# Seven-product blocks in all three down stages, their weight sums formed by accumulating DMAs in HBM

## The reference

```python
D_FF = 2816
...
        u_gate, u_val = jnp.split(u, 2, axis=-1)
        x = x + (jax.nn.silu(u_gate) * u_val) @ w_ffn_down[layer]
    return rms_norm(x, norm_final_w)
```

## Time and profile before

| | |
|---|---|
| median of 3 runs | 1244.31 us (1244.18 to 1244.35) |
| the profiled execution's own time | 1244.18 us |
| its span in the trace | 1242.9 us |
| PE busy | 1239.0 us, 100% of the span |
| DVE / ACT / POOL busy | 957.8 / 722.1 / 422.0 us (77% / 58% / 34%) |
| chain that ended last | PE 100% |
| DMA | 233.75 MB, 188 GB/s on average |

### The profile page before, as it was taken

One profiled execution on the slowest core, in us unless ns is written; L12 is line 12 of the kernel. 1 busy time (PEld: TensorE's weight loads), 2 busy tenths in 40 slices (PEclk: granted clock), 3 DMA queues, 4 the chain that ended last, 5 costly groups with the idle time before them and its releaser, 6 DMA issues.

```text
span 1242.9 us, 17085 instructions
## 1 busy us (share of the span) xinstructions
PE 1239.0 (100%) x6634; PEld 1061.2 (85%) x6634; DVE 957.8 (77%) x1377; ACT 722.1 (58%) x1023; POOL 422.0 (34%) x338
## 2 busy tenths in 40 slices
PE   9999999999999999999999999999999999999999
PEld 8988788888888889888888888888988888888887
DVE  6875667677887478986878888986898597888895
ACT  7755545376765365577836555546457674655552
POOL 0010012039892069377420112008746750012100
PEclk9999999999999999999999999999999999999999
DMA  9753334555555448644554554465855454555442
GB/s 360 274 195 136 136 119 169 173 199 187 197 179 201 170 170 267 214 155 176 175 210 175 183 190 162 176 220 185 289 180 193 154 174 165 203 183 190 162 166 114
DMA packets 39008, 233.75 MB, mean 188 GB/s; under 512 B 4752, under 2 KB 5392, under 8 KB 13072
## 3 DMA queue, kind: packets, MB, share of 16 engines
q1 hardware_dynamic: 38928, 232.67, 53.4%
HBM read 225.31 MB, written 1.05 MB: 182 GB/s over the span
## 4 chain that ended last, share of the span: by engine, by line
PE 100%; DVE 0%; issue 0%; POOL 0%; POOLq 0%
PE ps L657 19%; PE ps L564 18%; PE ps L566 18%; PE ps L565 18%; PE ps L662 10%; PE ps L569 6%; PE ps L583 2%; PE ps L625 1%; PE ps L624 1%; PE ps L623 1%; PE ps L725 1%; PE ps L1209 1%; PE ps L700 0%; PE ps L893 0%; PE ps L810 0%; PE ps L811 0%
## 5 line engine op out<-in xcount | busy, mean ns | idle before, releaser
L1299 ACT ACTIVATE whi<-raw 128x2048 fp32r<-128x2048 f32 (+1 forms) x212 | 400.2, 1891 | 115.0 <-PE ps L566 101.5
L2052 DVE TENSOR_TENSOR wlo<-raw,whi 128x2048 fp32r<-128x2048 f32 x168 | 388.0, 2315 | 90.0 <-ACT whi L1299 89.3
L1885 POOL TENSOR_TENSOR wlo<-raw,whi 128x512 fp32r<-128x512 f32 x176 | 229.1, 1337 | 88.6 <-ACT whi L1299 85.6
L657 PE MATMUL ps<-hh,whi 128*128 128x512 f32 x1056 | 255.8, 391 | 0.0
L657 PEld LDWEIGHTS ps<-hh,whi 128*128 128x128 f32 x1056 | 193.0, 188 | 36.5
L564 PE MATMUL ps<-whi,hh 128*128 128x512 f32 (+1 forms) x504 | 201.3, 399 | 0.0
L566 PE MATMUL ps<-whi,hh 128*128 128x512 f32 (+1 forms) x504 | 195.5, 388 | 0.0
L565 PE MATMUL ps<-wlo,hh 128*128 128x512 f32 (+1 forms) x504 | 195.1, 387 | 0.0
L1857 POOL TENSOR_TENSOR st<-st,sm 128x1 f32<-128x1 f32 (+2 forms) x28 | 45.2, 1614 | 391.5 <-DVE st L2106 228.0
L662 PEld LDWEIGHTS ps<-hh,wlo 128*128 128x128 f32 x1056 | 137.8, 191 | 6.7
L662 PE MATMUL ps<-hh,wlo 128*128 128x256 f32 x1056 | 139.8, 282 | 0.0
(11 more groups left out here) (348 smaller groups left out, 2061.6 us busy)
## 6 DMA issues: line engine op xcount, KB each, us to landing
raw<-in_w SPq DMA_DIRECT2D x202, 1024.0 KB, 4.9
raw<-in_w SPq DMA_DIRECT2D x12, 256.0 KB, 6.7
gain<-in_bias SPq DMA_DIRECT2D x12, 256.0 KB, 5.0
kst<-kh SPq DMA_DIRECT2D x16, 128.0 KB, 2.8
qst<-qh SPq DMA_DIRECT2D x16, 128.0 KB, 2.3
raw<-in_w SPq DMA_DIRECT2D x2, 560.0 KB, 10.8
x<-in_x SPq DMA_DIRECT2D x4, 256.0 KB, 5.7
gain<-in_rows SPq DMA_DIRECT2D x2, 512.0 KB, 5.6
```

Of the source, the lines that this page charges most:

```text
L657: pe.op.matmul(o[:, :], wh[:, k, c], t.hh[:, k, :, :], start=k == 0, stop=False, skip_group_check=True)
L1299: act.op.activation(t.whi[i % NHI][:, c], t.raw[i % NRAW][:, c], ACT.Copy).then_inc(*at("act_hi", ("hi", i)))
L1885: pool.op.tensor_tensor(t.wlo[i % NRAW][:, half(k)], t.raw[i % NRAW][:, half(k)], t.whi[i % NHI][:, half(k)].bitcast(F32), ALU.subtract).t ...
L2052: dve.op.tensor_tensor(t.wlo[i % NRAW][:, c], t.raw[i % NRAW][:, c], t.whi[i % NHI][:, c].bitcast(F32), ALU.subtract).then_inc(*at("dve_lo ...
```

## The change

`SEVEN` becomes a tuple for each stage: chunks 2, 3, 4, 6 in dn0 (none before), 1, 2, 4, 5 in dn1 (1, 3, 5, 7 before), 1, 2, 4, 5, 6, 7 in dn2 (1, 3, 5, 7 before). That makes 14 seven-product chunks in place of 8.

The sums chunks of c = 4 in dn1 and dn2 are still added by DVE (`BY_DVE`). The other 12 (`FORMED`) are built in HBM, in a new tensor `sums`, in two batches: the seven of dn0 and dn1 while the first model runs, the five of dn2 during layer 0 of the second. For each, SP copies 1 MB of weight blocks within HBM (`blocks_copied`, two DMAs, issued ahead of the loads of chunks 16 to 22, and of the five chunks from `pa0_0` on); then POOL issues four accumulating DMAs of 128 x 512 (`first_sums`, and `later_sums` in two steps, each of which waits for the one before to land). SP later loads the finished sums chunk like a weight chunk (`load_sums`), and of the chunk itself only the last 1536 columns.

In dn0 the sums of activations are formed by DVE (`block_sums`) and split by ACT and DVE, since POOL is splitting weights in up0; in dn1 and dn2 POOL forms them as before. `sevens_added` now runs in dn0 too. The cut diff (left out: hunks that only pass `SEVEN[n]` for `SEVEN`, or move a helper):

```diff
--- before.py
+++ after.py
@@ -36,6 +36,15 @@
             plan.append((name, layer, cs, k, per))
+
+    def down(unit, name, layer):
+        n = int(unit[2])
+        units[unit] = []
+        for c in range(NFT // 2):
+            units[unit].append(len(plan))
+            plan.append((name, layer, cols((512, 512), (0, 512)) if c in SEVEN[n] else cols((0, 1024)), 2 * c, 2))
+            if c in SEVEN[n]:
+                plan.append((None, n, range(1024), 2 * c, 2))
     def in1(unit, a, n):
...
@@ -76,16 +85,12 @@
             wide(f"up{l + 1}_{f}", "w_ffn_in_2", l, cols((128 * f, 128), (FF + 128 * f, 128)), 8, 8)
-        for c in range(NFT // 2):
-            halves = cols((512, 512), (0, 512)) if c in SEVEN else cols((0, 1024))
-            units.setdefault(f"dn{l + 1}", []).append(len(plan))
-            plan.append(("w_ffn_out_2", l, halves, 2 * c, 2))
-            if c in SEVEN:
-                plan.append((None, l, range(1024), 2 * c, 2))
+        down(f"dn{l + 1}", "w_ffn_out_2", l)
     return plan, units
-SEVEN = (1, 3, 5, 7)
+SEVEN = ((2, 3, 4, 6), (1, 2, 4, 5), (1, 2, 4, 5, 6, 7))
+BY_DVE = ((), (4,), (4,))
 GATES = (4, 5, 0, 1, 2, 3)
...
@@ -279,6 +285,10 @@
 SUMS = {i for i in range(len(PLAN)) if PLAN[i][0] is None}
+FORMED = [i for i in sorted(SUMS) if PLAN[i][3] // 2 not in BY_DVE[PLAN[i][1]]]
+BATCH = [[i for i in FORMED if (PLAN[i][1] == 2) == late] for late in (False, True)]
+COPIES = {a + n: i for a, batch in zip((16, UNITS["pa0_0"][0]), BATCH) for n, i in enumerate(batch)}
+OFFS = [sum(128 * PLAN[j][4] * len(PLAN[j][2]) for j in range(i) if j not in SUMS) for i in range(len(PLAN) + 1)]
@@ -383,7 +393,7 @@
     t.gs = at("gs", p + 82, [128, 4, 128])
-    t.gsh, t.gsl = ([at(f"{w}{c}", p + o + (4, 8, 40, 30)[c], [128, 4, 128], R32) for c in range(len(SEVEN))]
+    t.gsh, t.gsl = ([at(f"{w}{c}", p + o + (4, 8, 40, 34, 30, 0, 21)[c], [128, 4, 128], R32) for c in range(7)]
                     for w, o in (("gsh", 44), ("gsl", 46)))
@@ -444,22 +454,32 @@
     at, on = ev.at, ev.on
-    offs = [0]
-    for i in range(len(PLAN)):
-        offs.append(offs[-1] + (0 if i in SUMS else 128 * width(i)))
-
     def load(sem, dst, src, *names):
             sp.wait_ge(*on("used", i - NRAW))
-        src = d["in_w"][offs[i]:offs[i + 1]].rearrange("(p n) -> p n", p=128)
+        src = d["in_w"][OFFS[i]:OFFS[i + 1]].rearrange("(p n) -> p n", p=128)
         if i < 3:
             return
-        load(f"d_raw{i % NRAW}", t.raw[i % NRAW][:, 0:width(i)], src, ("raw", i))
+        c = slice(512 if i + 1 in FORMED else 0, width(i))
+        load(f"d_raw{i % NRAW}", t.raw[i % NRAW][:, c], src[:, c], ("raw", i))
+
+    def load_sums(i):
+        sp.wait_ge(*on("used", i - NRAW))
+        sp.wait_ge(*on("sums formed", int(i in BATCH[1])))
+        load(f"d_raw{i % NRAW}", t.raw[i % NRAW][:, :], d["sums"][FORMED.index(i)], ("raw", i))
+
+    def blocks_copied(i):
+
+
+        src = d["in_w"][OFFS[i - 1]:OFFS[i]].rearrange("(p n) -> p n", p=128)
+        for h in range(2):
+            load("d_copied", d["sums"][FORMED.index(i)][:, 1024 * h:1024 * h + 1024], src[:, 512 + 512 * h:1536 + 512 * h],
+                 *([("blocks copied", int(i in BATCH[1]))] * (h and i in (BATCH[0][-1], BATCH[1][-1]))))
     def row(i):
@@ -532,7 +552,11 @@
                 stack_q(l)
-        if i not in SUMS:
+        if i in COPIES:
+            blocks_copied(COPIES[i])
+        if i in FORMED:
+            load_sums(i)
+        elif i not in SUMS:
             load_raw(i)
@@ -1085,7 +1109,7 @@
         def seven(c):
-            i, pair, edge = chunks[c], SEVEN.index(c), (SEVEN[0], SEVEN[-1])
+            i, pair, edge = chunks[c], SEVEN[n].index(c), (SEVEN[n][0], SEVEN[n][-1])
             pe.wait_ge(*on("lo", i))
...
@@ -1626,9 +1653,8 @@
                 silu(f, "scaled")
-                if f % 2 == 0 and f // 2 - 2 in SEVEN:
-                    c = f // 2 - 2
-                    upper(("g sums hi", n, c), t.gsh[SEVEN.index(c)][:, :, :], t.gs[:, :, :], ("g sums", n, c, "whole"))
+                if f % 2 == 0 and f // 2 - 2 in SEVEN[n]:
+                    sums_upper(f // 2 - 2)
                 return
@@ -1638,6 +1664,8 @@
                                   bias=fc[:, f, v, 3:4]).then_inc(*at("act_out", *([("fu biased", f)] * v)))
+            if f % 2 and (f - 3) // 2 in SEVEN[n]:
+                sums_upper((f - 3) // 2)
         def second_sums(f):
...
@@ -1886,6 +1914,31 @@
                 *at("pool_lo", *([("lo", i)] if k == 3 else [])))
+
+    def added(sem, dst, src, *names):
+        pool.op.dma_start(dst, src, accum_op=ALU.add).then_inc(*at(sem, *names, by=16))
+
+    def first_sums(late):
+
+
+        pool.wait_ge(*on("blocks copied", late))
+        for i in BATCH[late]:
+            s = d["sums"][FORMED.index(i)]
+            first = d["in_w"][OFFS[i - 1]:OFFS[i]].rearrange("(p n) -> p n", p=128)[:, 0:512]
+            for j in range(2):
+                added("d_one", s[:, half(j)], first, *([("first sums", late)] * (j and i == BATCH[late][-1])))
+
+    def later_sums(late):
+
+
+        pool.wait_ge(*on("first sums", late))
+        for i in BATCH[late]:
+            s = d["sums"][FORMED.index(i)]
+            added("d_two", s[:, half(2)], s[:, half(0)], *([("second sums", late)] * (i == BATCH[late][-1])))
+        pool.wait_ge(*on("second sums", late))
+        for i in BATCH[late]:
+            s = d["sums"][FORMED.index(i)]
+            added("d_three", s[:, half(3)], s[:, half(2)], *([("sums formed", late)] * (i == BATCH[late][-1])))
     for tt in range(2):
@@ -1899,6 +1952,7 @@
             *at("pool_small", ("kr", "rot", tt)))
+    first_sums(0)
     for k in range(4):
@@ -1906,6 +1960,7 @@
                 *at("pool_small", ("sg gained", k - 1)))
+    later_sums(0)
     for tt in range(2):
@@ -1968,8 +2023,12 @@
             norm_power(norm_before_ffn, tt)
-        for c in SEVEN:
+        if l == 0:
+            first_sums(1)
+        for c in SEVEN[l + 1]:
             g_sums(l + 1, c)
+        if l == 0:
+            later_sums(1)
     def g_sums(n, c):
...
@@ -2044,7 +2103,7 @@
             dve.wait_ge(*on("raw", i))
-            if i + 1 in SUMS:
+            if i + 1 in SUMS and i + 1 not in FORMED:
                 weight_sums(i)
@@ -2575,10 +2634,28 @@
                 dve.wait_ge(*on("g", n, f - 4))
-                if n and f % 2 == 0 and f // 2 - 2 in SEVEN:
+                if n and f % 2 == 0 and f // 2 - 2 in SEVEN[n]:
                     dve.wait_ge(*on("g sums", n, f // 2 - 2, "whole"))
                 *at("dve_out", ("fg", n, f)))
+
+        def block_sums(c):
+
+
+            k0, k1 = (t.fg[(2 * c + k) % 4] for k in range(2))
+            a11, a21, a12, a22 = k0[:, 0:128], k0[:, 128:256], k1[:, 0:128], k1[:, 128:256]
+            s3, s5, s6, s7 = (t.gs[:, j, :] for j in range(4))
+
+            def less(dst, a, b, names=()):
+                dve.op.tensor_tensor(dst, a, b, ALU.subtract).then_inc(*at("dve_small", *names))
+
+            await_own("dve_out")
+            less(s5, a21, a22)
+            less(s7, a11, a21)
+            await_own()
+            less(s6, a11, s5)
+            await_own()
+            less(s3, a12, s6, [("g sums", n, c, "whole")])
         def up_out(f):
@@ -2587,6 +2664,12 @@
                 gated(f - late)
+            if n == 0 and f % 2 and (f - 3) // 2 in SEVEN[n]:
+                block_sums((f - 3) // 2)
+            if n == 0 and f % 2 == 0 and (f - 4) // 2 in SEVEN[n]:
+                c = (f - 4) // 2
+                lower([("g sums", n, c)], t.gsl[SEVEN[n].index(c)][:, :, :], t.gs[:, :, :],
+                      t.gsh[SEVEN[n].index(c)][:, :, :], ("g sums hi", n, c), "dve_small")
             if n and 0 <= f - late - 1 < NFT:
...
@@ -2996,6 +3079,7 @@
     out = nc.dram_tensor("out_0", (S, D), _mybir.dt.float32, kind="ExternalOutput").ap()
-    program(nc, {**d, "out": out})
+    sums = nc.dram_tensor("sums", (len(FORMED), 128, CW), _mybir.dt.float32, kind="Internal").ap()
+    program(nc, {**d, "out": out, "sums": sums})
     r = _run(nc, [arrays], core_ids=[0])```

What moves, engine by engine. POOL, between the rotation of `kr` (two rows on `ra`) and the powers of the norm `n1` (the two rows on 128x1), before and of the change; `st`, `sm`, `sg`, `gnw` are small tables of statistics and gains:

```order
L1900 TENSOR_TENSOR ra_113<-ra_113,rb_115 128x512
L1857 TENSOR_TENSOR st<-st,sm 128x2 x2
L1907 TENSOR_TENSOR sg<-sg,gnw 128x1024
L1857 TENSOR_TENSOR st<-st,sm 128x2
L1907 TENSOR_TENSOR sg<-sg,gnw 128x1024
L1857 TENSOR_TENSOR st<-st,sm 128x2
L1857 TENSOR_TENSOR st<-st,sm 128x1 x2
```

More of the change, by code:

```diff
@@ L60, in chunk_plan @@
         wide(f"up0_{f}", "w_ffn_up", 0, cols((128 * f, 128), (FF + 128 * f, 128)), 8, 8)
-    wide("dn0", "w_ffn_down", 0, cols((0, 1024)), NFT, 2)
+    down("dn0", "w_ffn_down", 0)
     for l in range(2):
@@ L111 @@
     "d_third0", "d_third1", "d_third2", "d_third3",
+    "d_copied", "d_one", "d_two", "d_three",
 )
@@ L1123, in ffn @@
```

(14 more changed lines are left out.)

## The result

The changed kernel takes 1254.18 us (median of five runs, 1253.47 to 1255.06), the kernel before 1244.18 us in the same session (1243.77 to 1244.35): ratio 1.008, 95% interval 1.0068 to 1.0091. It is 10 us slower, and 13.9 us above the forecast of 1240.3.

The account below looks back on a forecast made before the run. PE, busy 100% of the span, was taken as the bound: 4.08 us saved by 18 fewer matmuls, 0.1 lost in loads, from 1244.31 to 1240.3 us. Likeliest 1240.0 to 1240.9, 8 in 10 between 1239.8 and 1243.5.

Parts of the forecast that it names:

- Matmuls: Down stages: 18 fewer matmuls on PE, four chunks' worth in dn0, none in dn1, two in dn2, saving 4.08 us.
- DVE in up0: Four groups of new DVE instructions in up0, at most 2.4 us each time, 9.5 in all, at cost 0.
- The bound of 0.42 us: In up0, each DVE instruction of 128 x 128 was taken to last below 0.42 us.
- The warning: DVE and POOL already disturb each other in up0: DVE's split takes 2.61 us there against 2.29 in dn2.
- The rule of the Trainium skill: In up0, a DVE instruction with two SBUF inputs blocks a GpSimd instruction reading SBUF until it ends; still no PE wait.
- The cover in up0: DVE idles 19 and POOL 17 of up0's 111 us; even if POOL lost 9.5 us, PE would not wait.
- Rival D: In up0, DVE and POOL delays add up in blocks 7 to 12: up to 2 us, 1241 to 1242.5; chance 0.06.
- POOL's issues (B): POOL's accumulating DMAs: cost 0 taken; rival: up1's start late if issues exceed 3.4 us each, over 1246.8 us, chance 0.10.
- Copies (C): Copies within HBM at 57 to 103 us: cost 0 taken; rival: they starve loads, 1242 to 1247 us, chance 0.07.
- the sign that the prediction named for C: ACT waiting for `raw<-in_w` between 65 and 120 us would show copies within HBM starving the loads.
- Loads in the down stages (A): Sums chunks loaded in dn0 and dn2: 0.1 us lost; rival: late loads, 1241 to 1245 us, chance 0.15.
- The limit of 7.1 us: Time left for a sums chunk's landing in the worst cases, c = 4 in dn0, c = 6 and 7 in dn2.

Follow-up runs that it names:

- e6: The changed kernel with POOL's weight splits in up0 cut from 512 to 32 columns and PE reading the upper part instead of the remainder: 1241.05 us.
- e2: The changed kernel with DVE's sums of activations in up0 moved behind the sum and scaling of the next block, same work: 1247.33 us.
- e5: The changed kernel with up0's sums formed in unused PSUM, an added ACT copy, and DVE's split of the sums moved ahead of the convolution: 1241.57 us.
- e3: The changed kernel with three of the four groups of activation sums in up0 cut to one column of 128: 1250.37 us.
- e4: The changed kernel with dn0's seven-product chunks at c = 1, 3, 5, 7 in place of 2, 3, 4, 6: 1258.24 us.

## Why the prediction was wrong, point by point

**Matmuls: right.** 6616. With POOL out of the way (e6) dn0 takes from its first to its last matmul 57.8 us (60.5 before), dn1 57.8 (57.8), dn2 55.6 (56.9): 2.7 and 1.4 shorter.

**DVE in up0: the step that failed.** It put the four groups at "at most 2.4 us each time, 9.5 in all", and at a cost of 0. Measured are 18.6 us for the 16 subtractions and 2.7 for the four splits, 21.3 in all; DVE's groups of the changed kernel, 272 to 395 us:

```profile
L2650 DVE TENSOR_TENSOR gs<-fg,gs 128x128 f32<-128x128 f32 x8 | 9.6, 1195 | 0.3
L2650 DVE TENSOR_TENSOR gs<-fg 128x128 f32<-128x128 f32 x4 | 5.0, 1240 | 0.0
L2650 DVE TENSOR_TENSOR gs<-fg,fg 128x128 f32<-128x128 f32 x4 | 4.0, 992 | 0.1
```

The bound of 0.42 us is given to the earlier trace rows, which has no instruction below 128x512; it is what 128x256 takes in dn2, where POOL is idle. The warning was read in the earlier trace rows, but from the wrong instruction: a split of 2.3 us loses 0.3 to POOL, which looks like a seventh. The loss is a wait for each instruction, so it weighs on short ones: 0.87 us on each of 0.29. The `fg` product of up0 (a mean of 683 ns in the trace of the kernel before, single ones between 0.41 and 1.46 us) was the nearer measure, and it was not used.

The rule of the Trainium skill that the prediction took (page "SBUF — State Buffer", section "Who interferes with whom") was used in one direction only, DVE stopping POOL. The section also calls the shared ports an exclusive lock and says that issue order decides who blocks; the Trainium skill's rule for this pair (the same page, section "Summary: rules for kernel authors") is that the second one to issue is fully blocked until the first finishes. The runs agree with that half: 1181 ns for one column, 290 ns with POOL's pieces cut short, 300 ns with one input in PSUM.

**The cover in up0: wrong too.** The prediction set DVE's and POOL's idle time (19 and 17 us) against the work, and priced POOL's lateness alone. But DVE's order puts the sums ahead of the operation that ACT waits for. Little of DVE's idle time was free to use: its waits for the tile that ACT makes from the scaled block are 15.9 us before and still 14.6 after (272 to 395 us), and its whole idle time there fell only from 21.7 to 16.4 us, for 21.3 us of new work. The two engines handed each other's delay back and forth. The place alone is worth 6.9 us (e2), and operands in PSUM, with the subtractions still at the bad place, remove all of the loss but 1.2 us (e5). The two are not to be added: with the operands mended the place does nearly no harm. Shorter POOL pieces, with nothing moved, remove all but 0.7 (e6: 1241.05 against 1240.33), so the other terms of the sum were right to within that.

**Rival D named the right place and a sixth of the size.** It had "up to 2 us"; the stage lost over 12, by the two kernels that take that loss away (1254.2 against 1241.6 and 1241.05). What it lacked, besides the length of the subtractions, was that PE pays twice: in idle time (10.1 us), and in slower matmuls behind it (4.9, of which 3.4 by the lower clock).

**POOL's issues (B): the cost of 0 holds.** 14 accumulating DMAs took 11.95 us, 0.85 each, seven 5.91; the powers behind them still wait for DVE, as in the earlier trace rows. So does the first `gs` of up1 behind the ten that B was priced on, which took 8.44 us where 34.2 were covered:

```profile
103.19 11.95 POOL L1919 DMA_DIRECT2D sums<-in_w  x14 [23.05 <-DMA sums<-in_w]
...
174.33 0.72 POOL L1885 TENSOR_TENSOR st<-st,sm 128x2 f32<-128x2 f32 x1 [59.19 <-DVE st L2496]
...
216.31 5.85 POOL L1919 DMA_DIRECT2D sums<-sums  x7 [15.21 <-DMA sums<-sums]
259.75 0.57 POOL L1885 TENSOR_TENSOR st<-st,sm 128x1 f32<-128x1 f32 x1 [37.59 <-DVE st L2165]
...
679.02 8.44 POOL L1919 DMA_DIRECT2D sums<-in_w  x10
701.01 0.57 POOL L2041 TENSOR_TENSOR gs<-fg,fg 128x128 f32<-128x128 f32 x1 [13.55 <-DVE fg L2639]
```

POOL waited 15.2 us for the landing in the middle where 5 were taken, and there was room for it.

**Copies (C): the cost of 0 holds, with less in hand than reckoned.** The stretch of the earlier trace rows is full, and the sign that the prediction named for C is there: the eight loads issued in it land after 12.1 us in the median (5.0 before), and ACT waits for `raw<-in_w` three times, 6.5 us in all, longest 3.8. But it never reaches PE, which is busy throughout:

```profile
57.00:103.00 46.00, 46.00 (x250) 38.46 (x248) 33.01 (x43) 25.52 (x39) 4.57 (x2) 1.00 0.96 360
```

**Loads in the down stages (A): right in place and near in size.** The limit of 7.1 us for c = 7 of dn2 was met by a load of 7.75 us in one profile; PE lost 0.75 us, where 0.1 had been taken; in the changed kernel's own profile it took 6.96 us, with a wait of PE of 0.36 us behind it. Over the profiles of this study the same load was issued 4.8 to 7.8 us before ACT started on it, and PE's waits behind it cost nothing to 1.7 us. In dn0 none was late enough to show with POOL out of the way.

**What is left open.** Why the clock fell after some waits and not after others. In the changed kernel it fell after 3.06 and 2.26 us and stayed at 1.00 after 2.43 us at dn0's start; in e2 it stayed there after 3.07 us, but in e3 it fell to 0.66 over 4 us after 3.35 us at the same place. The length of the wait alone doesn't decide it. Open too are the shares of the 4 us by which e4 is worse.
